# A two-layer diffusion trunk on one Trainium2 core: sample slots turned ahead of the prompt rows, one token gather instead of two at the end of the output stage, and the first expert's tokens set between the first weight rows

## The reference

```python
def expert_choice_ffn(h, w_router, w_gate, w_up, w_down):
    B, T, D = h.shape
    cap = EC_CAPACITY * T // N_EXPERTS
    aff = jax.nn.softmax(jnp.einsum('btd,de->bte', h, w_router, preferred_element_type=jnp.float32), axis=-1)
    gate, idx = lax.top_k(aff.swapaxes(1, 2), cap)
    xg = jax.vmap(lambda hb, ib: hb[ib])(h, idx)
    a = jnp.einsum('becd,edf->becf', xg, w_gate)
    u = jnp.einsum('becd,edf->becf', xg, w_up)
    y = jnp.einsum('becf,efd->becd', jax.nn.silu(a) * u, w_down) * gate[..., None].astype(h.dtype)
    return jax.vmap(lambda yb, ib: jnp.zeros((T, D), yb.dtype).at[ib.reshape(-1)].add(yb.reshape(-1, D)))(y, idx)
```

## Time and profile before

| what | value |
|---|---|
| median of 3 runs | 4213.06 us (4207.27 to 4214.35) |
| the profiled execution's own time | 4200.83 us |
| its span in the profile | 4199.0 us |
| mean granted TensorE clock | 0.915 of full speed |
| PE busy | 3582.2 us, 85% of the span |
| DVE busy | 2326.6 us, 55% |
| ACT busy | 1701.2 us, 41% |
| POOL busy | 589.7 us, 14% |

### The profile page before, as it was taken

One profiled execution on the slowest core, in us unless ns is written; L12 is line 12 of the kernel. 1 busy time (PEld: TensorE's weight loads), 2 busy tenths in 40 slices (PEclk: granted clock), 3 DMA queues, 4 the chain that ended last, 5 costly groups with the idle time before them and its releaser, 6 DMA issues. The chain is left out here.

```text
span 4199.0 us, 56311 instructions
## 1 busy us (share of the span) xinstructions
PE 3582.2 (85%) x22440; PEld 2694.4 (64%) x22440; DVE 2326.6 (55%) x3515; ACT 1701.2 (41%) x2591; POOL 589.7 (14%) x499
## 2 busy tenths in 40 slices
PE   5969887998769999996899887429996679999995
PEld 1449855665646666664799765429995556666663
DVE  5133333334568788785312453545555667878884
ACT  2031155002346566663211166514434355656553
POOL 0020041221100010000300000025641101000000
PEclk8979998998879999998899998759997889999997
DMA  4132195514448887885442201343325458788885
GB/s 162 67 116 96 63 309 168 159 48 161 173 157 292 301 286 282 292 287 197 117 120 90 109 23 60 111 111 82 99 58 191 156 202 299 273 290 294 299 282 196
DMA packets 378504, 743.15 MB, mean 177 GB/s; under 512 B 99512, under 2 KB 222535, under 8 KB 377080
## 3 DMA queue, kind: packets, MB, share of 16 engines
q1 hardware_dynamic: 358906, 682.76, 46.6%
q0 software_dynamic: 16720, 56.41, 5.5%
q10 hardware_dynamic: 2618, 0.40, 0.1%
HBM read 634.01 MB, written 106.10 MB: 176 GB/s over the span
## 5 line engine op out<-in xcount | busy, mean ns | idle before, releaser
L2425 DVE TENSOR_TENSOR moe_w_low<-ffn_w,moe_w_high 128x1024 fp32r<-128x1024 f32 x768 | 897.7, 1219 | 77.9 <-ACT moe_w_high L2351 75.3
L2351 ACT ACTIVATE moe_w_high<-ffn_w 128x1024 fp32r<-128x1024 f32 x768 | 778.0, 1053 | 219.0 <-DMA ffn_w<-moe_w_gate 127.1
L2275 PE MATMUL moe_small<-ffn_w,ffn_xpT 128*16 128x512 f32 x2048 | 238.3, 594 | 0.0
L2255 PE MATMUL moe_G<-moe_w_high,moe_xT_high 128*128 128x512 f32 x512 | 185.4, 443 | 20.2 <-DVE moe_xT_low L2389 13.3
L224 PE MATMUL proj_mm<-proj_hT_low,proj_w_high 128*128 128x384 f32 x576 | 193.2, 335 | 0.0
L224 PE MATMUL proj_mm<-proj_hT_high,proj_w_low 128*128 128x384 f32 x576 | 193.1, 335 | 0.0
L224 PE MATMUL proj_mm<-proj_hT_high,proj_w_high 128*128 128x384 f32 x576 | 193.1, 335 | 0.0
L2949 PE MATMUL gdnc_a<-gdnc_T,gdnc_kg 128*128 128x64 f32 (+1 forms) x864 | 102.1, 267 | 87.8 <-ACT gdnc_T L2999 85.6
L224 PE MATMUL proj_mm<-proj_w_high,proj_hT_low 128*128 128x416 f32 (+1 forms) x504 | 176.0, 349 | 0.0
L224 PE MATMUL proj_mm<-proj_w_high,proj_hT_high 128*128 128x416 f32 (+1 forms) x504 | 175.5, 348 | 0.0
L224 PE MATMUL proj_mm<-proj_w_low,proj_hT_high 128*128 128x416 f32 (+1 forms) x504 | 174.6, 346 | 0.0
(11 more groups left out here) (479 smaller groups left out, 7437.3 us busy)
## 6 DMA issues: line engine op xcount, KB each, us to landing
ffn_w<-moe_w_gate SPq DMA_DIRECT2D x256, 512.0 KB, 6.4
ffn_w<-moe_w_up SPq DMA_DIRECT2D x256, 512.0 KB, 7.2
ffn_w<-moe_w_down SPq DMA_DIRECT2D x256, 512.0 KB, 5.6
attnrun_m_w<-w_ada SPq DMA_DIRECT2D x40, 1024.0 KB, 11.1
scratch_conv<-proj_zf POOLq DMA_DIRECT2D x24, 512.0 KB, 2.9
scratch_tm<-proj_tm SPq DMA_DIRECT2D x45, 208.0 KB, 2.0
scratch_spec<-front_room SPq DMA_DIRECT2D x36, 256.0 KB, 2.1
proj_w_raw<-even_w_in SPq DMA_DIRECT2D x24, 384.0 KB, 3.8
```

The costliest lines, as they stand in the source:

```text
L2255: mm = nc.tensor.matmul(bank[:, half, :], stat[a][:, k, :], cut[b][:, half * BANK:(half + 1) * BANK], start=k == 0 and i == 0, stop=k == K ...
L2275: nc.tensor.matmul(out, stat, w, start=k == 0, stop=k == KD - 1, tile_position=(0, 32 * q)).then_inc(small_done, 1)
L2351: nc.scalar.activation(w_high[n % CUT_ROOM][:], raw_rows(wall, n), ACT.Copy).then_inc(w_up, 1)
L2425: nc.vector.tensor_tensor(w_low[n % CUT_ROOM][:], raw_rows(wall, n), w_high[n % CUT_ROOM][:].bitcast(F32), ALU.subtract).then_inc(w_cut, 1)
```

## The change

In the output stage PE's two transposes of the sample slots stand ahead of the 16 transposes of the prompt rows, and POOL issues only expert 0's gather there. Expert 1's gather becomes POOL's first instruction of the expert stage. In the expert stage, DVE's two memsets move behind the first three weight tiles; ACT no longer waits for them, and PE waits for them only ahead of the first prompt products, which write the cleared bank. DVE sets the tokens' first half behind weight tile 0, the second behind tile 1, and cuts the halves behind the set of tile 1 and behind tile 2. ACT rounds them behind its second and third tile.

```diff
@@ mix_out, PE
+            pe.wait_ge(top_done, 1)
+            for n, src in enumerate((idxf, top)):
+                mm = nc.tensor.transpose(rt[0][:, n * E:(n + 1) * E], src[:, 0:CAP_S], keep.ident[0:E, 0:E])
+            mm.then_inc(slots_turned, 1)
             pe.wait_ge(xgp_in, 16 * (E // PG))
             for n in range(4):
...
-            pe.wait_ge(top_done, 1)
-            for n, src in enumerate((idxf, top)):
-                mm = nc.tensor.transpose(rt[0][:, n * E:(n + 1) * E], src[:, 0:CAP_S], keep.ident[0:E, 0:E])
-            mm.then_inc(slots_turned, 1)
@@ mix_out, POOL
             pool.wait_ge(slots_set, 1)
-            for e in range(2):
-                tokens.fetch(nc, io, keep, e)
+            tokens.fetch(nc, io, keep, 0)
@@ experts, POOL
+            fetch(1)
             for e in range(2, 4):
@@ experts, PE
             def small_rows(e, ks, down):
+                if not down and ks[0] == 0 and e == 0:
+                    pe.wait_ge(cleared, 1)
...
                 turn_tokens(0, i)
-            pe.wait_ge(cleared, 1)
@@ experts, ACT
-            act.wait_ge(cleared, 1)
...
-                if n in (2, 3):
-                    round_first(n - 2)
+                if n in (1, 2):
+                    round_first(n - 1)
@@ experts, DVE
-            nc.vector.memset(small_bank[:], 0.0)
-            nc.vector.memset(sgp[:], 0.0).then_inc(cleared, 1)
             for n, (e, m, k) in enumerate(order):
+                if n == 3:
+                    nc.vector.memset(small_bank[:], 0.0)
+                    nc.vector.memset(sgp[:], 0.0).then_inc(cleared, 1)
                 dve.wait_ge(w_up, n + 1)
                 nc.vector.tensor_tensor(w_low[n % CUT_ROOM][:], ...).then_inc(w_cut, 1)
-                if n == 2:
-                    for i in range(NF):
-                        set_tokens(0, i)
-                        cut_first(i)
+                if n < NF:
+                    set_tokens(0, n)
+                if 1 <= n <= NF:
+                    cut_first(n - 1)
```

## The result

| | before | after |
|---|---|---|
| median of the comparison | 4211.72 us (6 runs, 4201.87 to 4214.35) | 4186.06 us (6 runs, 4180.14 to 4191.93) |
| ratio, 95% interval | | 0.9943 (0.993 to 0.9956) |
| a second comparison | 4207.28 us (16 runs) | 4184.00 us (5 runs), ratio 0.9948 (0.9935 to 0.9962) |
| profiled span | 4199.0 us | 4184.2 us |

By the two ratios the kernel became 24 us (18.5 to 29.5) and 22 us (16 to 27) faster.

What follows compares the result with a forecast made beforehand. The prediction took PE to bound the expert stage, with both seams on the path to the end. Savings of 12.8 + 3.8 = 16.6 us off the median of 4213.06 gave 4196.5 us, range 4189 to 4206.

Steps and rivals of the forecast that it cites:

- sum of 16.6 us: Output stage's end and expert stage's start, both layers: 12.8 + 3.8 us saved.
- The seam: End of the output stage: release comes 6.36 us earlier in layer 0 and 6.4 in layer 1, 12.8 in all.
- the slots' place: Output stage: PE turning the slots ahead of the prompt rows is worth 5.2 us per layer.
- The start: Start of the expert stage: covered rounding wait 0.64 and earlier ACT 1.24, together 1.9 us per layer.
- What was put at nothing: Expert stage: moved gather of expert 1, later weight cuts and later memsets (`cleared`) each cost 0.
- the clock: Expert stage: PE's half-speed stretches, 2.4, 1.7, 3.0 and 0 us, kept as is, bounds +3 and −3 us.
- Rival 1: Expert stage: clock rises before the first products, expert 1's hole costs nothing; 7.1 us more, 4189.4; chance 0.08.
- the base: Whole kernel: the saving was taken off the median of 4213.06 us, not the profiled execution's 4200.83.

Runs made afterwards that it cites:

- hole_before: The kernel before with 12 dense products of present tiles on PE in the idle gap ahead of expert 1's first product; ratio 0.9989.
- shift4: The changed kernel with four extra clears of unused tiles on DVE ahead of the first token cut; 4186.90 us in one run.
- shift6: The changed kernel with six extra clears of unused tiles on DVE ahead of the first token cut; 4193.44 us in one run.
- hole_after: The changed kernel with 12 dense products of present tiles on PE ahead of expert 1's first product; ratio 0.9944 against the kernel before.
- startfill_after: The changed kernel with three products of present tiles on PE between expert 0's transposes and its first product; ratio 0.9956.

## Why the prediction was wrong

**Right.** Its sum of 16.6 us is the path's measured 16.6, and by its terms, not by luck. The seam came to 6.3 us per layer (forecast 6.4): POOL drains 0.3 us behind the one gather's landing, and ACT releases the stage. Within it the slots' place gave 4.9 instead of 5.2. The start gave 1.97 us per layer (forecast 1.9), with ACT at 0.10 us behind the release. What was put at nothing cost nothing: there is no wait for a weight cut, for `cleared`, or for the moved gather, though that one took 6.2 us to land beside SP's row loads. POOL's two gathers at the stage's start still took 0.94 us each beside DVE's work.

**Wrong in the clock.** "None of it follows from the program's text ... I keep it as is, with +3 and −3 us as bounds" was the step that failed. It took the four slow stretches of one profile for chance about a fixed mean. The kernel before was slow behind the hole in five of six stages; its one profile shown ahead had the one exception in layer 1. The changed kernel was slow in none of six. That term measured −5.5 us (2 × 2.7), outside its bounds of 3. It also counted only windows near the two gaps, and took the length of a window for that of the slow stretch: in layer 0 the clock stayed at 0.50 for 5.2 us behind the first product (0.57 over 6 us), not 4.83. The fall at the stage's end was not in it. Rival 1 was of this kind and went too far: the slow stretch at the first product remained, 3.1 to 3.7 us. The time was 3 us lower still than its 4189.4, which its mechanism alone does not give (see the base below). Against an earlier rise the prediction set the transposes at 0.50; they showed that the clock had not risen yet, not that it would rise no sooner.

**In part the base.** The saving was taken off 4213.06, a median of three. Later medians of the same kernel were 4206.65 (29 runs), 4207.28 (16) and 4205.74 (11). Against the first of these the forecast was 6.4 us too high before any term. Base and clock together are then 6.4 + 5.5 = 11.9 us, and the miss was 10.4. This share is an estimate: the later medians come from other occasions and three chips, and in the first comparison itself the kernel before stood at 4211.72 (6 runs), 1.3 us under the base. The saving alone, 24 or 22 us against 16.6, misses by 5 to 7, and that is the clock's term within the intervals.

**Open.** What sets the instant at which the clock rises, and so whether the changed kernel owes its six clean holes to its shorter path or in part to luck. That the clock, and not another cause, makes the loss behind the hole is shown by hole_before. That the path's length decides the clock is not shown: shift4 speaks for it, shift6 and hole_after speak against it. Why the stage's end differs by 1.5 to 2 us between stages with a full clock behind the hole is open too.

## What to carry to other kernels

At a stage border look at what each engine's drain waits for: here POOL's held the whole core until its gathers had landed, and a gather that isn't needed at once belongs behind the border. In a body bound by TensorE an idle hole in TensorE's work can have two prices, the hole itself and a slower clock behind it (in 12 of 26 stages here), and the second can come out otherwise after an edit elsewhere; read the granted clock over several profiles before taking it as fixed. A saving is to be set against a base of many runs, or given as a ratio.

## What the runs showed of the hardware that was not expected

Dense work in an idle gap did not keep the clock through the next gap. In both layers of startfill_after, full clock at the first product (1.00 instead of 0.69 to 0.74) went with a fall in the next hole (0.73 and 0.74) that the changed kernel without filler did not have. The kernel before's second gather landed 5.1 us after its issue behind another, a lone one 4.2, and one issued beside the row loads 6.2 (5.8 in layer 1). POOL's drain at the stage's end lasted until its gathers had landed: 6.8 to 7.3 us with two of them, 4.6 to 5.3 with one.
